# Two phases with seven block products in both for the squared-ReLU MLP of a decoder layer

## The reference

```python
hf = rms_norm(x, norm_mlp[l])
x = x + jnp.square(jax.nn.relu(hf @ w_up[l])) @ w_down[l]
return rms_norm(x, norm_final)
```

## Time and profile before

| | |
|---|---|
| time, median of 3 runs (lowest, highest) | 2840.79 us (2839.5, 2841.35) |
| the profiled execution's own time | 2839.88 us |
| its span, first to last instruction | 2838.2 us |
| mean granted TensorE clock over the span | 0.998 |
| PE busy | 2808.7 us (99%) |
| DVE busy | 1597.4 us (56%) |
| ACT busy | 1012.1 us (36%) |
| POOL busy | 403.7 us (14%) |
| first matmul of the MLP, about | 1513 us |
| last matmul, about | 2828 us |

### The profile page before, as it was taken

One profiled execution on the slowest core, in us unless ns is written; L12 is line 12 of the kernel. 1 busy time (PEld: TensorE's weight loads), 2 busy tenths in 40 slices (PEclk: granted clock), 3 DMA queues, 4 the chain that ended last, 5 costly groups with the idle time before them and its releaser, 6 DMA issues.

```text
span 2838.2 us, 33822 instructions
## 1 busy us (share of the span) xinstructions
PE 2808.7 (99%) x12777; PEld 2321.5 (82%) x12777; DVE 1597.4 (56%) x2058; ACT 1012.1 (36%) x1370; POOL 403.7 (14%) x254
## 2 busy tenths in 40 slices
PE   8999999999999999999999999999999999999998
PEld 7888888888788888888878888888888888888886
DVE  5222245454335556532344577776777777767776
ACT  6222234343232223322344333334333344333334
POOL 1000000000000001000000322332233223313330
PEclk9999999999999999999999999999999999999999
DMA  7323232332333232543212233233223322332232
GB/s 269 104 93 100 89 104 103 103 103 104 104 119 104 74 111 97 190 165 104 89 60 87 77 119 103 91 104 118 90 88 117 118 84 93 118 118 77 101 119 104
DMA packets 132034, 306.27 MB, mean 108 GB/s; under 512 B 7561, under 2 KB 7674, under 8 KB 129530
## 3 DMA queue, kind: packets, MB, share of 16 engines
q1 hardware_dynamic: 130522, 294.80, 31.0%
q10 hardware_dynamic: 1440, 10.49, 0.9%
HBM read 290.58 MB, written 14.68 MB: 108 GB/s over the span
## 4 chain that ended last, share of the span: by engine, by line
PE 97%; DVE 1%; ACT 1%; issue 0%; DMA 0%; SPq 0%; POOL 0%; POOLq 0%; DVEq 0%; ACTq 0%
PE acc L1668 16%; PE acc L1670 16%; PE acc L1669 16%; PE acc L1994 8%; PE acc L1993 8%; PE acc L1992 8%; PE aux L2012 7%; PE aux L2014 7%; PE aux L2016 7%; PE aux L1689 1%; PE aux L1779 1%; PE aux L1762 0%; PE aux L1761 0%; PE aux L1771 0%; PE acc L2034 0%
## 5 line engine op out<-in xcount | busy, mean ns | idle before, releaser
L1013 DVE TENSOR_TENSOR wlo<-raw,whi 128x2048 fp32r<-128x2048 f32 x128 | 293.3, 2291 | 490.9 <-ACT whi L610 489.8
L1668 PE MATMUL acc<-act_hi,whi 128*128 128x512 f32 x1088 | 432.4, 397 | 0.5 <-DVE act_lo L1017 0.5
L1670 PE MATMUL acc<-act_hi,wlo 128*128 128x512 f32 x1088 | 425.0, 391 | 0.0
L1669 PE MATMUL acc<-act_lo,whi 128*128 128x512 f32 x1088 | 424.1, 390 | 0.0
L1446 DVE TENSOR_TENSOR flo<-wide,fhi 128x1024 fp32r<-128x1024 f32 x188 | 257.7, 1372 | 253.2 <-ACT fhi L884 253.2
L610 ACT ACTIVATE whi<-raw 128x2048 fp32r<-128x2048 f32 x128 | 244.5, 1910 | 435.7 <-PE acc L1670 427.4
L1992 PE MATMUL acc<-act_hi,fhi 128*128 128x512 f32 x1024 | 398.7, 389 | 0.0
L1994 PE MATMUL acc<-act_hi,flo 128*128 128x512 f32 x1024 | 398.4, 389 | 0.0
L1993 PE MATMUL acc<-act_lo,fhi 128*128 128x512 f32 x1024 | 398.4, 389 | 0.0
L884 ACT ACTIVATE fhi<-wide 128x1024 fp32r<-128x1024 f32 x188 | 199.4, 1061 | 525.0 <-PE acc L1994 364.8
L2012 PE MATMUL aux<-fhi,P_hi 128*128 128x512 f32 x840 | 326.8, 389 | 0.2 <-DVE xs L1505 0.2
(11 more groups left out here) (313 smaller groups left out, 4159.8 us busy)
## 6 DMA issues: line engine op xcount, KB each, us to landing
raw<-in_w_in SPq DMA_DIRECT2D x80, 1024.0 KB, 5.1
raw<-in_w_up SPq DMA_DIRECT2D x64, 1024.0 KB, 5.3
wide<-in_w_down SPq DMA_DIRECT2D x64, 1024.0 KB, 5.2
raw<-in_w_out SPq DMA_DIRECT2D x16, 1024.0 KB, 5.1
gates_scratch<-gate_out ACTq DMA_DIRECT2D x10, 1024.0 KB, 3.9
raw<-in_w_ckv SPq DMA_DIRECT2D x8, 1024.0 KB, 11.5
xs<-in_x SPq DMA_DIRECT2D x8, 1024.0 KB, 12.8
raw<-in_w_attn_br SPq DMA_DIRECT2D x8, 1024.0 KB, 8.2
```

Of the source, the lines that this page charges most:

```text
L1013: nc.vector.tensor_tensor(wlo[n % 2][:], raw[n % 4][:], whi[n % 2][:].bitcast(F32), ALU.subtract).then_inc(lo_ready, 1)
L1668: nc.tensor.matmul(dst, s_hi, v_hi, start=first, stop=False)
L1669: nc.tensor.matmul(dst, s_hi, v_lo, start=False, stop=False)
L1670: ins = nc.tensor.matmul(dst, s_lo, v_hi, start=False, stop=last)
```

## The change

The MLP now runs in two phases. First all of the up product is computed, in 16 blocks of 512 features, each as seven products over halves of tokens, width and features; then all of the down product, in 15 blocks of seven products and a plain one for the last. The activations between the phases go through DRAM (`hid_dram`), already split into hi and lo and already summed into the seven operands. The residual x goes to DRAM (`x2_dram`) before the up phase and comes back behind it.

A block has 14 units (two for each product). An up unit is 24 matmuls with 256 moving columns (half of the tokens); a down unit is 12 with 512. The order of products is P1, P2, P6, P7, P5, P4, P3, so units 0 and 1 are P1, 4 and 5 are P6, and so on. Four of the eight weight sums of a block are GpSimd's, for P7 and P6 (up) or P5 and P6 (down); four are DVE's (`late_mixes`), for P5 and P3 (up) or P7 and P4 (down). During an up block DVE and ACT also make ReLU, square, sums and splits of the block before, and SP stores them. The 128x1024 units, the ring of four and the three float32r matmuls for each product are as they were.

The diff, cut to what sets the order of the work (in order: constants; `up_mixes` of GpSimd; `unit_split_hi` of ACT; the functions of DVE down to `down_block`; `up_unit` and `down_unit` of PE):

```diff
-WITH_UP = ("P1", "U", "P2", "P6", "U", "P7", "P5", "U", "P4", "P3", "U")
+UNITS = 14
+N_UP = 16
+N_BLOCKS = 32
+OPERANDS = ("P1", "P4", "P2", "P5", "P6", "P7", "P3")
+OPERANDS_Q7 = ("P1", "P4", "P2", "C12", "P5", "P6", "P7", "P3")
+OPERAND_POS = {"P1": 0, "P4": 1, "P2": 2, "C12": 3, "P5": 4, "P6": 5, "P7": 6, "P3": 8}
+STAGES = 3
...
+        def up_mixes(b):
+            for u in range(2):
+                pool.wait_ge(unit_lo, b.of(UNITS, u + 1))
+                pool.wait_ge(raw_loaded[2], b.of(16, 512 + 16))
+                mixed(nc.gpsimd.tensor_tensor(half_slot(0, u), half_slot(0, u), half_slot(2, u), ALU.subtract))
+                pool.wait_ge(raw_loaded[3], b.of(16, 512 + 16))
+                pool.wait_ge(mix_w_ready, b.of(4, 2 * u + 1))
+                mixed(nc.gpsimd.tensor_tensor(mix[u][:], half_slot(3, u), half_slot(0, u), ALU.subtract))
...
+        def unit_split_hi(b, n, down):
...
+                act.wait_ge(unit_used, b.of(UNITS, n - RING + 1))
+            nc.scalar.activation(fhi[ring(b, n)][:], unit_source(down, n), ACT.Copy).then_inc(unit_hi, 1)
...
+        def unit_split_lo(b, n, down):
+            dve.wait_ge(unit_hi, b.of(UNITS, n + 1))
+            nc.vector.tensor_tensor(flo[ring(b, n)][:], unit_source(down, n), fhi[ring(b, n)][:].bitcast(F32),
+                                    ALU.subtract).then_inc(unit_lo, 1)
...
+        def hidden(b, name):
...
+            nc.vector.tensor_tensor(c[:], bank[:], add[:], ALU.add).then_inc(dve_read, 1)
+            dve.wait_ge(dve_read, b.of(4, k + 1))
+            nc.vector.scalar_tensor_tensor(out=c[:], in0=c[:], scalar=0.0, in1=c[:], op0=ALU.max, op1=ALU.mult).then_inc(hid_ready, 1)
+        def hidden_last(b):
+            dve.wait_ge(act_read, b.of(4, 4))
+            nc.vector.tensor_tensor(c12[:], c12[:], c12[:], ALU.mult).then_inc(dve_read, 1)
...
+        def operand_lo(b, name):
+            dve.wait_ge(side_hi, operands_before(b, name) + 1)
+            nc.vector.tensor_tensor(staged[st][:, 1], operand_source[name][:], staged[st][:, 0].bitcast(F32),
+                                    ALU.subtract).then_inc(side_lo, 1)
+        def late_mixes(b, n, down):
+            first, second = (4, 7) if down else (5, 6)
+            if n == first:
+                dve.wait_ge(mix_w_ready, b.of(4, 4))
+                for u in range(2):
+                    slot, op = (1, ALU.subtract) if down else (2, ALU.add)
+                    nc.vector.tensor_tensor(half_slot(slot, u), half_slot(3, u), half_slot(slot, u), op).then_inc(mix_d_ready, 1)
+            if n == second:
+                dve.wait_ge(unit_lo, b.of(UNITS, n + 1))
+                for u in range(2):
+                    out, a = (half_slot(2, u), half_slot(2, u)) if down else (mix[u][:], half_slot(1, u))
+                    nc.vector.tensor_tensor(out, a, mix[u][:], ALU.subtract).then_inc(mix_d_ready, 1)
+        def before_unit(b, n):
+            if n == 1:
+                hidden(b, "C21")
+            if n == 3:
+                hidden_last(b)
+                hidden_sum(b, "S1")
+                hidden_sum(b, "S2")
+        def behind_unit(b, n):
+            for name in operand_list(b):
+                if OPERAND_POS[name] == n:
+                    operand_lo(b, name)
+            if n == 3:
+                hidden_sum(b, "S3")
+            if n == 5:
+                hidden_sum(b, "S4")
+        def up_block(b):
+            for n in range(UNITS):
+                if not first:
+                    before_unit(b.next(-1), n)
+                if n == 7:
+                    hidden(b, "C11")
+                if n == 13:
+                    hidden(b, "C22")
+                if not first or n >= RING:
+                    unit_split_lo(b, n, False)
+                late_mixes(b, n, False)
...
+                if not first:
+                    behind_unit(b.next(-1), n)
...
+        def down_block(b):
+            for n in range(UNITS):
+                if first:
+                    before_unit(chunk, n)
+                elif n in (1, 3):
+                    land(b.next(-1), {1: "P4", 3: "P3"}[n])
+                if n in (5, 7, 9, 11, 13):
+                    land(b, PRODUCTS[(n - 5) // 2])
+                unit_split_lo(b, n, True)
+                late_mixes(b, n, True)
+                if first:
+                    behind_unit(chunk, n)
...
+        def up_unit(b, n, hooks=None):
...
+            for m in range(2):
+                bank = up_bank(b, name)[:, 256 * m:256 * (m + 1)]
+                for i in range(4):
+                    k = 4 * u + i
+                    nc.tensor.matmul(bank, w_hi[:, i, cols(m)], x_hi[:, k, :], start=name in UP_FRESH and n % 2 == 0 and m == 0 and i == 0,
+                                     stop=False, skip_group_check=True)
+                    nc.tensor.matmul(bank, w_hi[:, i, cols(m)], x_lo[:, k, :], start=False, stop=False, skip_group_check=True)
+                    ins = nc.tensor.matmul(bank, w_lo[:, i, cols(m)], x_hi[:, k, :], start=False, stop=u == 1 and i == 3,
+                                           skip_group_check=True)
...
+        def down_unit(b, n):
...
+                if p >= 2:
+                    pe.wait_ge(pair_free, b.of(7, p - 1 - 7 * N_UP))
```

More of the change, by code:

```diff
@@ new lines, in down_block, with next_side @@
+        def down_block(b):
+            d = b.first - N_UP
+            sides_free = d % 2 and (not isinstance(b.turn, int) or b.of(1) < N_BLOCKS - 4)
+            i = (d // 2) % 2
+            q = ds(b.turn * 2 + (d // 2 + 2), 1) if sides_free else None
+            def next_side(pi):
+                if sides_free:
+                    load_side(i, q, PRODUCTS[pi], b.of(UNITS, 2 * pi + 2))
+            next_side(0)
+            next_side(1)
+            for slot, lo, pi in ((1, 8, 2), (0, 10, 3), (2, 12, 4), (3, 14, 5)):
+                load_down(slot, b.next(), unit_lo, b.of(UNITS, lo))
+                next_side(pi)
+            next_side(6)
@@ new lines, in _ @@
+        for p in range(2):
+            up_block(Block_no(N_UP // 2 - 1, 2, p))
+        for e in range(4):
+            down_block(Block_no(0, 4, N_UP + e))
+        with act.Fori(1, 3) as r:
+            for e in range(4):
+                down_block(Block_no(r, 4, N_UP + e))
+        for e in range(3):
+            down_block(Block_no(3, 4, N_UP + e))
+        last = Block_no(0, 2, N_BLOCKS - 1)
+        for n in range(8):
+            act.wait_ge(raw_loaded[n // 2], last.of(16, 512 + 16))
+            act.wait_ge(unit_used, last.of(UNITS, n - RING + 1))
+            nc.scalar.activation(fhi[ring(last, n)][:], half_slot(n // 2, n % 2), ACT.Copy).then_inc(unit_hi, 1)
@@ new lines, in down_block @@
+        def down_block(b):
+            first = isinstance(b.turn, int) and b.of(1) == N_UP
+            chunk = Block_no(0, 2, N_UP - 1)
+            for n in range(UNITS):
+                if first:
[8 more added lines that the diff above has]
+                    behind_unit(chunk, n)
@@ new lines, in plain_step @@
+        def plain_step(m, j, n, k0):
+            w_hi, w_lo = (f[ring(last, n)][:].rearrange("p (k n) -> p k n", k=2) for f in (fhi, flo))
+            for i in range(2):
+                a_hi, a_lo = plain_side(m, k0 + i)
+                bank = z_bank(m, j)[:]
+                nc.tensor.matmul(bank, a_hi, w_hi[:, i, :], start=k0 + i == 0, stop=False, skip_group_check=True)
+                nc.tensor.matmul(bank, a_hi, w_lo[:, i, :], start=False, stop=False, skip_group_check=True)
+                ins = nc.tensor.matmul(bank, a_lo, w_hi[:, i, :], start=False, stop=k0 + i == 7, skip_group_check=True)
+            return ins
@@ L2066, in _ @@
         for m in range(NT):
[L2067 to L2070 removed]
             for z in range(4):
[L2072 to L2073 removed]
                 if m == 0:
[L2075 to L2081 removed]
+                    pe.wait_ge(unit_lo, last.of(UNITS, 4 + z + 1))
```

928 lines of the change are left out of this document (494 added, 434 removed).

## The result

| kernel | median us | runs | ratio to before, 95% |
|---|---|---|---|
| before | 2840.25 (2839.5 to 2841.35) | 4 | |
| after | 2925.47 (2924.96 to 2928.14) | 4 | 1.0302 [1.0284, 1.0319] |

The change makes the kernel slower by 3.0%. The forecast was 2883, in a range of 2815 to 2908: the sign was right, the size was not. The spans of the two profiled executions are 2838.2 and 2923.6 us, 85.4 apart, where the forecast had 43.3.

What follows compares the result with a forecast made beforehand. PE's number of matmuls was taken to bound the kernel, with DVE behind it. 2839.9 - 53.4 (PE) + 61.6 (blocks 1 to 14) + 5.0 (15) + 7.8 (16) + 10.5 (17 to 30) + 11.8 (0) = 2883 us; range 2815 to 2908.

Steps and rivals of the forecast that it cites:

- PE's term: Up phase: 3072 matmuls (695.8 us) give way to 5376 with 256 columns (642.4 us); PE saves 53.4 us.
- the stalls of blocks 1 to 14: Up blocks: PE waits for DVE's late lo parts, 4.4 us in each block, 61.6 us in all.
- block 0: First up block: DVE's extra sums and lo parts of x come late, PE loses 11.8 us (2 to 16).
- blocks 16 and 17, to the third mark: Change from up to down: the prediction's steps give three periods of 43.9, 40.4 and 38.8 us between DVE's late sums.
- 12 other down blocks: Down blocks 17 to 30: PE waits 0.75 us each for P1's landing, 10.5 us in all; 38.8 us a block.
- block 16's walk: First down block: lo(3), P1's landing and P6's landing come late for units 3, 4 and 8; 7.8 us (0 to 12).
- PE's price of a narrow matmul: Up phase: a matmul with 256 columns costs PE 0.1195 us, from ten rows at the kernel's start.
- rival 3: Up phase: narrow matmuls pay for their 0.19 us weight load, 379 us more for PE, 3200 us; chance 0.01.
- the turns: DVE and GpSimd instructions with two SBUF inputs never run at once; one GpSimd sum holds DVE for 2.27 us.
- Rival 1: DVE keeps up and PE's saving stays: 0 to 0.5 us an up block, 2809 us (2795 to 2832); chance 0.19.
- Hidden, at nothing: loads and stores: Loads and stores cost nothing: 176 GB/s needed against 269 seen; a load lands in 5.3 us, issued 11 ahead.
- Rival 2: Memory is late at the change of phase or all along: up to 20 us on top, 2903 us; chance 0.08.

Runs made afterwards that it cites:

- e1: Kernel after, with GpSimd's four weight sums of a block cut to 16 of 1024 columns (results not the reference's); 2833.2 us, ratio 0.9975.
- e3: Kernel after, with all eight weight sums of a block on DVE and none on GpSimd; 2860.0 us, ratio 1.0067.
- e5: Kernel after, with the first three operand stores at the change of phase issued ahead of three side loads and x's second half; 2918.65 us, ratio 1.0275.
- e8: Kernel after, with the down blocks' side loads of P5 and P4 issued behind the weight loads of slots 2 and 3; 2920.7 us, ratio 1.0281.
- e9: Kernel after, with e5's store order and block 18's seven side loads issued behind the loads of blocks 17 and 18; 2910.9 us, ratio 1.0245.
- e4: Kernel after, with DVE's `low_sums(0)` at the MLP's start moved behind all four additions to the residual; 2921.8 us.
- e10: Kernel after: e3's sums, P3's behind unit 8; e4's additions first, x's lo parts nearer use; orders of e5, e8, e9; 2811.3 us, ratio 0.9897.
- e7: Kernel before, with GpSimd's four weight sums of a set cut to 16 of 512 columns in each row; 2839.4 us, ratio 0.9997.
- e2: Kernel after, with DVE's four late weight sums of a block cut to 16 of 1024 columns (results not the reference's); 2874.9 us, ratio 1.0121.

## Why the prediction was wrong

The gap between the spans is 85.4 us, the forecast's 43.3; 42 are missing. By its own steps:

| step | forecast us | measured us | off |
|---|---|---|---|
| PE's term and the stalls of blocks 1 to 14 (a block) | 44.55 | 44.48 | -1.0 in 14 |
| block 0 | 11.8 lost | 22.4 lost | +10.6 |
| blocks 16 and 17, to the third mark | 123.1 | 146.3 | +23.2 |
| 12 other down blocks (a block) | 38.8 | 39.69 | +10.7 |

The last column adds up to 43.5, 1.4 more than are missing. The forecast's 123.1 holds a slip of half a microsecond: in block 16's walk unit 3 is put at 16.3 us, but the three units ahead of that block are up units of 2.87 us, which makes it 16.8 and the block's stall 7.3 in place of 7.8.

**What held.** PE's price of a narrow matmul, from ten rows at the start of the kernel, held (0.1195 us, measured 0.12), and rival 3 is out: weight loads of 0.19 us don't space these matmuls. The sentence of the Trainium skill weighed there (TensorE: Matmul & The Clock Gate, Part 3, The mechanism) has no support in the up phase either. It isn't all that the section says: it also has a weight load pulled ahead when it goes to the background weight buffer, which the prediction left out and which the 0.12 us doesn't contradict. The walk through DVE's order, instruction by instruction with the turns, gave the period of an up block to 0.1 us, the two waits of PE and their places. The turns as their cause are shown by e1 and e3; the square of `hidden` takes part in them (2.27 against 0.69). Rival 1 (DVE keeps up) would be true without GpSimd: e1's 40.3 us.

**What failed.** It is the step "Hidden, at nothing: loads and stores". It compared bytes per block with the bandwidth of another slice, and one load's landing with the lead of its slot. In the mean neither was crossed: the loads of w_up land in 9.4 us, not in 5.3, but within the 11. It did not walk the queue, as DVE's had been walked. Two things were in the code to be read: that a store which frees a staging place stands behind 7 MB of loads (21.4 us of ACT's wait; by e5 11.5 us in one period, 7.9 over the three), and that in the down blocks slot 3's weights come behind operand loads (4.8 us by e8). A third, side loads issued well ahead of their use, cost 9.3 (e9). Rival 2 had the place and the size ("up to 20 us on top", at the change of phase, measured 23.2); whether its mechanism, the amount of bytes, has a share is not shown, since e9 moved the order too. It was to decide by the landing of a weight load, and first in the way stood a store. It got 0.08 because it was tested against a load's 5.3 us alone. It also stood beside the forecast instead of in its sum: with 2903 for it and 2908 as the upper end, no room was left for it together with a surplus elsewhere, which is what came.

**The term that was mis-sized** is block 0's. Its walk began at PE's start of unit 0 and left out what stands in DVE's queue ahead of that: `low_sums(0)` in front of additions on which PE's transposes wait. e4 shows it for 6.6 of the 10.6 us, at block 1's mark; where the other 4.0 come from is open. The clock of 0.82 in these 47 us is part of the same price, since with PE kept at work it is 0.93 (e4, the same stretch), and 1.00 in the first ten.

**Down blocks**: of the 0.9 us a block too little, e8 takes away 0.5, the alternating part (39.69 to 39.18); the 39.03 of the short ones is 0.2 over the forecast and goes with GpSimd's sums (38.08 in e1 and e3), as the step had it.

Still open: 4.0 us of block 0's surplus and the 11 us that e10 still loses there; 6.0 us of the change of phase, and how much of its price is the clock; and whether the amount of bytes bounds it at all. For that speaks only the DMA share of 1.00 in e5; a run with fewer bytes was not made.

## What to carry to other kernels

Before work is shared out between DVE and GpSimd, look for DVE rows of twice or four times their usual length beside POOL rows: there an instruction on GpSimd holds DVE for as long as it runs, and where DVE is near its limit it is cheaper for DVE to do it all (e3: 65 us less with four sums more). The lock costs nothing as long as DVE has the slack (e7), so it is to be priced anew whenever the bound moves to DVE. A lower clock behind a short stop of PE costs time only where PE is the bound (e2), so it can turn up when another wait is mended. A DMA queue is an engine like the others: walk it in order at every change of phase, with each store that frees a buffer in its place; a mean of GB/s hides a 512 KB store behind 7 MB of loads.

## What the runs showed of the hardware

The turns of DVE and GpSimd take in an instruction that has the same SBUF tile as both inputs: 2.27 us instead of 0.69, while the one before it, with an input in PSUM, keeps 0.69. The Trainium skill (SBUF — State Buffer, Who interferes with whom) has the rule, that DVE instructions with two SBUF inputs contend with GpSimd's reads of SBUF and those with at most one, outside the 2-port modes, don't, and this trace agrees.

All eight sums on DVE leave it no busier than four (357.3 us of 400 in e3, of 1800 to 2200, against 362.3 in after), with 9.7 blocks in that time against 9.0.

16 DMA engines were at a share of 1.00 with 394 GB/s over 40 us, with loads and stores mixed (e5); before, no slice of the kernel was above 269.

The granted clock fell behind PE's long stops: 0.82 in the stretch of block 0, where PE first waits 7.4 us with hardly any work around it, 0.80 in that of the change of phase with its stop of 18 us. Behind stops of 2 us it fell in some executions and not in others: from 1800 to 2200 us the mean is 1.00 in after, but 0.96 in e4 and 0.97 in e5, with the same stops twice in a block. What that costs depends on the bound. In e4 and e5, where DVE bounds, blocks behind such a fall take 44.4 to 44.7 us like the others; in e2, where PE is the bound for most of a block, 43.9 against 42.4.
